# The first norm's scales join the tokens, in three pieces on two queues; ten warm-up products; one product for a channel sum

## The reference

```
xn = x * rsqrt(mean(x*x) + eps) * norm1_g
h  = x + ( sigmoid(g_conv) * ConformerConv(xn @ w_in ...) + sigmoid(g_attn) * DilatedAttn(xn @ w_in ...) ) @ mix_w_out
hn = rmsnorm(h, norm2_g)
y  = h + PEER(hn)        # 8 heads, 2 x 128 sub-keys, top 16, all 16384 experts as u @ hn, gelu * gate, @ v
```

## Time and profile before

| | |
|---|---|
| median of 3 runs | 997.36 us (996.97 to 997.46) |
| the profiled execution, its own time | 997.07 us |
| its span, first to last instruction | 995.2 us |
| mean granted TensorE clock | 1.000 |
| busy share of PE, DVE, ACT, POOL | 99%, 78%, 51%, 47% |
| DMA | 181.95 MB, mean 183 GB/s |

### The profile page before, as it was taken

The page is one execution under the profiler, slowest core; times in us unless marked ns, Lnnn a source line. Parts: engine busy times, 40 slices in busy tenths (PEclk is TensorE's granted clock), DMA queues, the critical chain, the costliest instruction groups (busy, mean ns, idle before and its releaser), DMA issues.

```text
span 995.2 us, 21854 instructions
## 1 busy us (share of the span) xinstructions
PE 989.8 (99%) x7822; PEld 917.0 (92%) x7822; DVE 774.9 (78%) x1304; ACT 506.8 (51%) x789; POOL 465.3 (47%) x198
## 2 busy tenths in 40 slices
PE   9999999999999999999999999999999999999998
PEld 9998999999999999999999999888888888888887
DVE  5999784868899996097777777988888876776764
ACT  6663877544555544544444444444444445554443
POOL 3664366656689999874444444100000004344442
PEclk9999999999999999999999999999999999999999
DMA  6684445654455565555555555555554555556562
GB/s 242 211 308 150 149 148 162 212 201 149 150 197 200 171 211 188 191 176 184 177 180 174 182 172 169 185 175 170 177 180 171 182 174 190 190 189 195 186 203 90
DMA packets 52619, 181.95 MB, mean 183 GB/s; under 512 B 5943, under 2 KB 9155, under 8 KB 52452
## 3 DMA queue, kind: packets, MB, share of 16 engines
q1 hardware_dynamic: 52292, 181.16, 54.4%
q10 hardware_dynamic: 288, 0.27, 0.1%
HBM read 180.33 MB, written 3.43 MB: 185 GB/s over the span
## 4 chain that ended last, share of the span: by engine, by line
PE 93%; DVE 5%; ACT 1%; issue 0%; POOL 0%; ACTq 0%; DVEq 0%; POOLq 0%
PE bank L1218 50%; PE bank L1527 35%; DVE bank L798 3%; PE bank L1476 3%; PE bank L1319 1%; PE bank L1233 1%; PE bank L1451 1%; DVE lo L354 1%; PE bank L1242 1%; PE bank L1553 1%; PE bank L1335 1%; ACT hi L335 0%; PE bank L1358 0%; PE bank L1346 0%; PE bank L1249 0%
## 5 line engine op out<-in xcount | busy, mean ns | idle before, releaser
L354 POOL TENSOR_TENSOR lo<-raw,hi 128x1024 fp32r<-128x1024 f32 x184 | 462.4, 2527 | 515.9 <-ACT hi L335 515.4
L335 ACT CAST hi<-raw 128x1024 fp32r<-128x1024 f32 x332 | 348.0, 1049 | 218.0 <-PE bank L1527 186.3
L1218 PE MATMUL bank<-norm_space,hi 128*128 128x256 f32 x2624 | 452.4, 278 | 0.2 <-POOL lo L354 0.2
L1218 PEld LDWEIGHTS bank<-norm_space,hi 128*128 128x128 f32 x2624 | 396.2, 188 | 1.8 <-issue 1.2
L1218 PE MATMUL bank<-norm_space,lo 128*128 128x256 f32 x1312 | 362.8, 277 | 0.0
L1527 PE MATMUL bank<-hi,norm_space 128*128 128x512 f32 x1008 | 273.8, 391 | 0.0
L1218 PEld LDWEIGHTS bank<-norm_space,lo 128*128 128x128 f32 x1312 | 246.4, 188 | 0.0
L1527 PEld LDWEIGHTS bank<-hi,norm_space 128*128 128x128 f32 x1008 | 188.0, 188 | 38.5
L354 DVE TENSOR_TENSOR lo<-raw,hi 128x1024 fp32r<-128x1024 f32 x148 | 189.2, 1279 | 27.4 <-ACT hi L335 27.3
L1527 PE MATMUL bank<-lo,norm_space 128*128 128x512 f32 x504 | 155.5, 390 | 0.0
L1145 DVE TENSOR_TENSOR norm_space<-act,norm_space 128x256 fp32r<-128x256 f32 x128 | 111.7, 876 | 48.8 <-ACT norm_space L665 48.8
(11 more groups left out here) (183 smaller groups left out, 651.5 us busy)
## 6 DMA issues: line engine op xcount, KB each, us to landing
raw<-u_tiles SPq DMA_DIRECT2D x128, 512.0 KB, 3.3
raw<-v_tiles SPq DMA_DIRECT2D x128, 512.0 KB, 3.3
raw<-front SPq DMA_DIRECT2D x76, 512.0 KB, 3.8
toeplitz<-bias_row SPq DMA_DIRECT2D x6, 384.0 KB, 7.5
bias<-toeplitz SPq DMA_DIRECT2D x12, 128.0 KB, 3.5
resid<-x_t SPq DMA_DIRECT2D x2, 512.0 KB, 4.7
qk<-sub_keys SPq DMA_DIRECT2D x1, 1024.0 KB, 8.0
y<-act SPq DMA_DIRECT2D x3, 256.0 KB, 2.0
```

The costliest lines, as they stand in the source:

```text
L335: act_e.copy(hi[:, s, :], raw[:, s, :]).then_inc(hi_ready, 1)
L354: eng.tensor_tensor(lo[:, s, :], raw[:, s, :], hi[:, s, :].bitcast(F32), ALU.subtract)\
L1218: ins = pe.matmul(dst, w_[:, s, u * P:(u + 1) * P], x_[:, k, :], start=first and i == 0 and p_ == 0, stop=last and i == n - 1 and p_ == 2)
```

## The change

The gains `norm1_g` become the first eight columns of the token array, in DRAM and in SBUF (`x_space`). It is loaded in three pieces, on two queues: ACT's queue brings the gains with blocks 0 and 1 and then blocks 2 and 3; SP's queue brings weight tile 0 first, then blocks 4 to 7, then tiles 1, 2 and so on. ACT makes `xg_hi` of blocks 0, 1, 4, 5, 6, DVE that of 2, 3 and 7. ACT rounds tile 0 in two halves, between blocks 1 and 4. In `by_dve`, of tiles 0 to 3 only tile 1 is left to DVE; POOL writes `lo` of 0, 2 and 3. PE makes 10 warm-ups, takes tile 0's first products block by block with one more product of ones after each of blocks 0 to 5, and interleaves tiles 0 and 1. For each of the four channel sums DVE adds the last two blocks, and PE makes one product.

```diff
-WARM_UP = 27
+WARM_UP = 10
-XG_ACT = 5
+XG_ACT = (0, 1, 4, 5, 6)
+X_CHUNKS = ((0, 2), (2, 4), (4, 8))
-        resid = tmp("resid", [P, KB, T])
+        x_space = tmp("x_space", [P, KB + KB * T])
+        norm1_g, resid = x_space[:, 0:KB], x_space[:, KB:].rearrange("p (k t) -> p k t", t=T)
         def by_dve(base, j):
-            if base + j < 2:
-                return True
+            if base + j < RING:
+                return base + j == 1
+        def load_x(eng, i):
+            first, end = X_CHUNKS[i]
+            columns = slice(KB + first * T if i else 0, KB + end * T)
+            eng.dma_start(x_space[:, columns], x_t[:, columns]).then_inc(x_in[i], 16)
 (SP)
-            for r in range(2):
-                sp.dma_start(resid[:, 4 * r:4 * r + 4, :], x_t[:, 4 * r:4 * r + 4, :]).then_inc(x_in[r], 16)
             for g in range(N_FRONT):
                 load(front[g], g, 0, 0)
+                if g == 0:
+                    load_x(sp, 2)
 (ACT)
-            a.dma_start(prm[:, C_N1:C_N1 + KB], cols[:, C_N1:C_N1 + KB]).then_inc(gain_in, 16)
+            load_x(a, 0)
+            load_x(a, 1)
             a.preload_act_table(ACT.Sqrt)
+            a.wait_ge(x_in[0], 16)
+            x_hi(0)
+            x_hi(1)
+            wait_raw(a, 0, 0, 0)
+            a.copy(hi[:, 0, 0:D // 2], raw[:, 0, 0:D // 2]).then_inc(hi_first, 1)
+            a.copy(hi[:, 0, D // 2:D], raw[:, 0, D // 2:D]).then_inc(hi_ready, 1)
+            a.wait_ge(x_in[2], 16)
+            for k in XG_ACT[2:]:
+                x_hi(k)
+            split_hi(a, 1, 0, 0)
+            split_hi(a, 2, 0, 0)
+            a.wait_ge(x_in[1], 16)
+            a.activation(sq[:, 0:4, :], resid[:, 0:4, :], ACT.Square).then_inc(squared, 1)
+            squares(0)
             split_hi(a, 3, 0, 0)
+            squares(1)
             split_hi(a, 4, 0, 0)
 (DVE)
+            for k in range(KB):
+                (wait for the piece that block k opens)
+                if k not in XG_ACT:
+                    dve.tensor_scalar(xg_hi[:, k, :], resid[:, k, :], norm1_g[:, k:k + 1], None, ALU.mult)\
+                       .then_inc(xhi_dve, 1)
+                    dve.wait_ge(xhi_dve, own_parts)
+                x_lo(k)
-            lo_of(0)
             lo_of(1)
             (two additions of squares)
-            lo_of(3)
             (third addition)
+            dve.wait_ge(pair_sums, 3)
+            dve.tensor_tensor(sq[:, 0, :], sq[:, 0, :], sq[:, 1, :], ALU.add).then_inc(pair_sums, 1)
 (DVE, alike for lnsum, lnvar and ssq2)
+                    dve.tensor_tensor(sq[:, CB, :], sq[:, CB, :], sq[:, CB + 1, :], ALU.add).then_inc(acc_pairs, 1)
 (PE)
             def high_products(b, n, blocks=range(KB)):
+                for k in blocks:
+                    if n == 0 and k < KB // 2:
+                        pe.wait_ge(hi_first, 1)
+                    else:
+                        pe.wait_ge(hi_ready, n + 1)
                     pe.wait_ge(xlo, k + 1)
                     (two products)
+                    if n == 0 and k < KB - 2:
+                        keep_warm()
             def first_tiles():
-                high_products(b0, 0)
-                high_products(b1, 1)
+                high_products(b0, 0, range(KB - 1))
+                high_products(b1, 1, range(3))
+                high_products(b0, 0, range(KB - 1, KB))
+                high_products(b1, 1, range(3, KB))
                 low_products(b0, 0)
                 low_products(b1, 1)
                 high_products(b2, 2)
                 low_products(b2, 2)
                 b = start(("ssq1",))
-                pe.wait_ge(pair_sums, 3)
-                (two products)
+                pe.wait_ge(pair_sums, 4)
+                step(pe.matmul(b[:, 0:T], ones[:, :], sq[:, 0, :], start=True, stop=True))
 (PE, alike for lnsum, lnvar and ssq2: one product where there were two)
 (host)
-        "x_t": a["x"][0].T.reshape(KB, P, T).transpose(1, 0, 2),
+        "x_t": np.concatenate([col(a["norm1_g"][0]), a["x"][0].T.reshape(KB, P, T)...reshape(P, KB * T)], axis=1),
```

More of the change, by code:

```diff
@@ L473, in bias_rows, with x_hi, squares @@
                 a.copy(p3[0:HEADS, h, :], bank[BANK_OF[("bias", h)]][0:HEADS, 0:BW]).then_inc(act_evac, 1)
-            a.dma_start(prm[:, C_N1:C_N1 + KB], cols[:, C_N1:C_N1 + KB]).then_inc(gain_in, 16)
+            load_x(a, 0)
+            load_x(a, 1)
             a.preload_act_table(ACT.Sqrt)
[L477 to L487, removed]
+            def x_hi(k):
+                a.activation(xg_hi[:, k, :], resid[:, k, :], ACT.Copy, scale=norm1_g[:, k:k + 1]).then_inc(xhi, 1)
+            def squares(i):
                 a.activation(bank[6 + i][:, :].rearrange("p (k t) -> p k t", t=T), resid[:, 4 + 2 * i:6 + 2 * i, :],
                              ACT.Square).then_inc(squared, 1)
+            a.wait_ge(x_in[0], 16)
[12 more added lines that the diff above has]
+            squares(0)
             split_hi(a, 3, 0, 0)
+            squares(1)
             split_hi(a, 4, 0, 0)
@@ L734, in x_lo @@
             def x_lo(k):
-                dve.wait_ge(xhi, k + 1)
-                i, gain = k % KB, (C_N1, C_N2)[k // KB] + k % KB
-                dve.scalar_tensor_tensor(out=xg_lo[:, i, :], in0=resid[:, i, :], scalar=prm[:, gain:gain + 1],
+                i = k % KB
+                if k >= KB:
+                    dve.wait_ge(xhi, len(XG_ACT) + i + 1)
+                elif k in XG_ACT:
+                    dve.wait_ge(xhi, XG_ACT.index(k) + 1)
+                gain = prm[:, C_N2 + i:C_N2 + i + 1] if k >= KB else norm1_g[:, i:i + 1]
+                dve.scalar_tensor_tensor(out=xg_lo[:, i, :], in0=resid[:, i, :], scalar=gain,
                                          in1=xg_hi[:, i, :].bitcast(F32), op0=ALU.mult, op1=ALU.subtract)\
                    .then_inc(xlo, 1)
[L742 to L745, removed]
-                x_lo(k)
[L747 to L750, removed]
-            lo_of(0)
+            own_parts = 0
+            for k in range(KB):
+                for i, (first, _) in enumerate(X_CHUNKS):
+                    if k == first:
+                        dve.wait_ge(x_in[i], 16)
+                if k not in XG_ACT:
+                    own_parts += 1
+                    dve.tensor_scalar(xg_hi[:, k, :], resid[:, k, :], norm1_g[:, k:k + 1], None, ALU.mult)\
+                       .then_inc(xhi_dve, 1)
+                    dve.wait_ge(xhi_dve, own_parts)
+                x_lo(k)
             lo_of(1)
@@ L1231, in _, with keep_warm, high_products @@
             pe.wait_ge(const, 2)
+            def keep_warm():
+                pe.matmul(bank[5][:, 0:P], ones[:, :], ones[:, :], start=True, stop=True)
             for _ in range(WARM_UP):
-                pe.matmul(bank[5][:, 0:P], ones[:, :], ones[:, :], start=True, stop=True)
+                keep_warm()
             pe.wait_ge(const, 7)
-            def high_products(b, n):
-                pe.wait_ge(hi_ready, n + 1)
-                for k in range(KB):
+            def high_products(b, n, blocks=range(KB)):
+                for k in blocks:
[3 more added lines that the diff above has]
+                        pe.wait_ge(hi_ready, n + 1)
                     pe.wait_ge(xlo, k + 1)
@@ L1262, in first_tiles @@
                 b = start(("ssq1",))
-                pe.wait_ge(pair_sums, 3)
-                for k in range(2):
-                    ins = pe.matmul(b[:, 0:T], ones[:, :], sq[:, k, :], start=k == 0, stop=k == 1)
-                step(ins)
+                pe.wait_ge(pair_sums, 4)
+                step(pe.matmul(b[:, 0:T], ones[:, :], sq[:, 0, :], start=True, stop=True))
             def two_tiles(jobs, tiles, parts_ready, vec_hi, vec_lo):
@@ L1390, in _ @@
                     b = start(("lnsum",))
-                    pe.wait_ge(acc_pairs, 1)
-                    for k in range(2):
-                        ins = pe.matmul(b[:, 0:T], ones[:, :], sq[:, CB + k, :], start=k == 0, stop=k == 1)
-                    step(ins)
+                    pe.wait_ge(acc_pairs, 2)
+                    step(pe.matmul(b[:, 0:T], ones[:, :], sq[:, CB, :], start=True, stop=True))
                 if n == LNVAR_AT:
                     b = start(("lnvar",))
-                    pe.wait_ge(acc_pairs, 2)
-                    for k in range(2):
-                        ins = pe.matmul(b[:, 0:T], ones[:, :], sq[:, CB + k, :], start=k == 0, stop=k == 1)
-                    step(ins)
+                    pe.wait_ge(acc_pairs, 4)
+                    step(pe.matmul(b[:, 0:T], ones[:, :], sq[:, CB, :], start=True, stop=True))
                 if n == min(TURN_AT):
@@ L1428, in _ @@
             b = start(("ssq2",))
-            pe.wait_ge(square_run, KB - 2)
-            pe.wait_ge(squared, 3 + KB)
-            pe.matmul(b[:, 0:T], ones[:, :], sq[:, 0, :], start=True, stop=False)
-            step(pe.matmul(b[:, 0:T], ones[:, :], sq[:, KB - 1, :], start=False, stop=True))
+            pe.wait_ge(square_run, KB - 1)
```

(1 more changed line is left out.)

21 lines of the change are left out of this document (14 added, 7 removed).

## The result

The changed kernel takes 1012.57 us (1007.15 to 1013.49, 6 runs) against 996.92 us before (996.22 to 997.46, 6 runs): a ratio of 1.0149, 95% interval 1.0135 to 1.0163. That is 15.6 us slower. The forecast was slower by 7.4, within 995.5 to 1007.5.

What follows compares the result with a forecast made beforehand. PE, busy 99% of the span, was taken as the bound. `ssq1` ending at 27.6 instead of 19.02 us gives +8.6, the other sums -1.2: +7.4 on 997.07, so 1004.5 us, range 995.5 to 1007.5.

Steps and rivals of the forecast that it cites:

- DVE beside POOL: At the start, a DVE instruction with two SBUF operands waits out POOL's `lo`: one per `lo`, 2.4 to 2.6 us.
- Arrivals: Start loads: piece 0 lands at 5.7 us, tile 0 at 5.6, pieces 1 and 2 at about 7.8.
- the count of slots: Start: how many POOL `lo` from tile 2 on each let only one DVE instruction through; forecast three.
- POOL never idle until 19.3: Start: tile 4's `hi` is ready at 16.1, so POOL works without a gap from 11.6 to about 19.3 us.
- The clock: PE's burst after block 7 may start at 1.2 GHz, losing 0 to 2.65 us; the middle, 1.3, was taken.
- The gained sums: `lnsum`, `lnvar`, `ssq2` each lose a product, 0.4 us apiece, -1.2 in all; their new DVE additions are hidden.
- the six products between blocks lie in PE's idle time: Start of PE: the added products of ones after blocks 0 to 5 were taken to cost nothing.
- (a): Start: fewer slots, `ssq1` ends at 22.1 to 24.6, total 999 to 1004 us; chance 0.18.
- (b): Start evens out: all `x_lo` done before POOL asks for tile 2; 996.3 to 999 us; chance 0.13.
- (c): Faster: POOL's `lo` does not hold DVE at the start; 993.8, up to 996 us; chance 0.21.
- three slots: Forecast case at the start: DVE held behind POOL's `lo` of tiles 2, 3 and 4; 1002 to 1007.5 us; chance 0.48.

Runs made afterwards that it cites:

- late_pool: Changed kernel, but POOL's first `lo` waits until all eight `x_lo` are written: 1006.09 us, ratio 1.0094.
- a_again: The changed kernel once more, without an edit; its trace is of a long execution: 1012.42 us, ratio 1.014.
- sums_only: Kernel before plus one product for all four channel sums, nothing else: 996.92 us, ratio 1.0001.
- pe_start_only: Kernel before plus PE's side of the new start (10 warm-ups, new product order, products of ones between blocks): 999.98 us, ratio 1.0034.
- one_more_product: Changed kernel plus one identity product behind the first u tile: 1006.35 us, ratio 1.0097.
- three_mended: Changed kernel with POOL's first `lo` after all eight `x_lo`, two products for `lnvar`, an identity product behind the first u tile: 998.71 us, ratio 1.0015.
- pieces_pe: Changed kernel with `lo` of tiles 0 and 3 back on DVE and two products for every sum: 1005.82 us, ratio 1.0088.
- sums3_break: Kernel before plus one product for each sum except `lnvar`, and an identity product ahead of wq tile 3: 996.04 us, ratio 0.999.

## Why the prediction was wrong, point by point

The direction and the main mechanism were right, the time was not: 1012.57 lies 5.1 us above the range.

- **DVE beside POOL**: right. The held instructions took 2.37 to 2.6 us where 2.4 to 2.6 was forecast, one for each `lo` of POOL (`x_lo` of blocks 4 and 5, where 5, 6 and the scaling of 7 were named), and `late_pool` showed that this alone is 6.3 us.
- **Arrivals**: late by 0.2 to 0.7 us. Piece 0 was there at 6.3 against 5.7, tile 0 at 6.2 against 5.6, pieces 1 and 2 at 8.5 and 8.0 against 7.8. It cost no slot by itself, since the count of slots went by POOL; it did put the scaling of block 2 under POOL's first `lo`, as forecast.
- **POOL never idle until 19.3**: wrong, and the step of the sum that failed in the start. `hi` of tile 4 was set at 16.1 from its load alone, but ACT writes into the ring's slot only when PE has done tile 0: 23.10. POOL had no fourth `lo`, and `x_lo` of block 7 ended at 18.34, not 20.0.
- **The clock, 1.3 (0 to 2.65)**: right in kind, at the far end in size. From 18.34 the 52 products and the sum would end at 24.70 at full speed and ended at 27.06: 2.4 us. In `late_pool` it is 2.35 (12.03 + 6.36 = 18.4 against 20.76). Not all of it is the clock by itself: PE also comes late to the 52 products, with a product of ones at 0.43 us ahead of them (18.08), and with all six on its way where DVE is not held. The two errors nearly cancel, hence `ssq1` at 27.06 (27.5 in `a_again`) for 27.6: that the start came out so close is luck.
- **The gained sums, -1.2**: `lnsum` and `ssq2` gave 0.4 each. For the addition at `lnvar` the text named the danger ("could be caught by POOL, up to 1.96") and took nothing; it was caught, 2.51 us, and PE lost 1.35 net of the product saved. The term should have been +0.5, not -1.2. `sums_only` shows it alone, and a row of before would have told it, as POOL was busy in that stretch before the change (three `lo`, 8.54 us from 128.92). That the six products between blocks lie in PE's idle time held only where PE waits for DVE; in `pe_start_only` they cost PE 1.9 us.
- **Everything behind the start moves as it is**: never written down, and the step that put the time out of the range. In 8 of 10 executions, by their times and one trace, the u tiles run at 118 ns a product instead of 113, 6.4 us. Without it the forecast's own terms, corrected, give 8.5 + 0.5 = +9.0, 1006, within the range; the long executions are at +15.5 in their trace. `one_more_product`, at 1006.35, and `three_mended` show the cost. No row of before made it foreseeable at this place, though its wq tiles already ran at the wider spacing.
- **The rivals.** (a) and (b) needed POOL to come late; it came at 8.36, 11.87. (b) is what `late_pool` makes by hand, and even there the 2.35 us of the slow clock and the products of ones put tile 3 at +1.7, near the upper end. (c) fell with the held `x_lo`. The range for three slots alone, 1002 to 1007.5, was wider than its own terms, which with 0 to 2.65 for the clock give 1003.5 to 1006.1 as a median; nothing was named for the rest.

What decides the spacing of a stretch stays open. Shown is that it is constant from one break in PE's stream to the next, that a product of another kind can change it within one execution, and that its odds at the u tiles depend on how the program came there. Five waits instead of one left three of four executions long, which is too few to tell a small effect from none. Not shown is in what PE differs between the two.

## What to carry to other kernels

Before handing DVE's work to POOL, or putting an instruction with operands in SBUF on DVE, read what POOL does in that very stretch: beside a running 2.4 us `lo` a 0.35 us scaling, a 0.48 us `x_lo` and a 256-column addition each take 1.9 to 2.6 us, and one such addition cost what three saved products had won. A product that is to fill PE's idle time costs its full length where PE turns out not to wait. Before setting when an engine gets its next work, list every condition of that work, the release of its slot by the consumer among them, not only its load. When a small change moves the total, compare the tile rate in stretches that nothing touched: a uniform 4% on PE looks like nothing in the list of waits.

## What the runs showed of the hardware

The same 128x256 product with a 128x128 weight has two spacings in an unbroken stream at a granted clock of 1.00: 113 and 118 ns, 1061 and 1021 in 120 us. The spacing holds for 60 tiles (170 us) and was seen to change only at breaks: at the change from 64 small products to the u tiles, or behind one identity product. In `one_more_product` and `three_mended` the u tile ahead of the identity product runs at 118 ns and those behind it at 113, in the same execution. At the entry to the u tiles the gap from the last small product is 194 ns in `a_again` as in before, and only what follows differs. The spacing explains the two groups of times of the changed kernel, 1007 and 1012.5, of which both have a trace, and fits those of `pieces_pe`, 999.6 and 1006, and of `sums3_break`, 994.7 and 996.2 (13 tiles), of which only the shorter has one. Shorter stretches at 118 ns are in the trace of before as well: its wq tiles 3 to 15 (173 instructions from 220 to 240 us).
